# A hybrid decoder layer on one core: who scales the probability rows of head 2 in three units

## What is computed

```
p_c = masked_softmax(s_c, ...); o_cmp = einsum('bgqrc,bcgd->bgqrd', p_c, v_c)
p_s = masked_softmax(s_s, ...); o_slc = einsum('bgqrm,bgqmd->bgqrd', p_s, v_g)
p_w = masked_softmax(s_w, ...); o_win = einsum('bgqrk,bkgd->bgqrd', p_w, v_wb)
o_nsa = gates[..., 0:1] * o_cmp + gates[..., 1:2] * o_slc + gates[..., 2:3] * o_win
o_nsa = o_nsa * silu(nsa_z)
return x + einsum('bse,ed->bsd', concatenate([o_nsa, o_conv]), w_out)
```

## Time and profile before

| | us |
|---|---|
| median of 3 runs | 653.49 |
| lowest to highest | 653.38 to 653.90 |
| profiled execution | 654.13 |
| its span | 652.3 |
| PE busy in the span | 640.4 |
| DVE, ACT, POOL busy | 485.5, 378.1, 201.8 |

### The profile page before, as it was taken

One profiled execution on the slowest core, in us unless ns is written; L12 is line 12 of the kernel. 1 busy time (PEld: TensorE's weight loads), 2 busy tenths in 40 slices (PEclk: granted clock), 3 DMA queues, 4 the chain that ended last, 5 costly groups with the idle time before them and its releaser, 6 DMA issues.

```text
span 652.3 us, 10319 instructions
## 1 busy us (share of the span) xinstructions
PE 640.4 (98%) x3513; PEld 539.4 (83%) x3513; DVE 485.5 (74%) x1153; ACT 378.1 (58%) x872; POOL 201.8 (31%) x220
## 2 busy tenths in 40 slices
PE   9999999999999999999999999998999999999997
PEld 6889998888888888888888888886888878788876
DVE  4945979996755754776698867898887778787853
ACT  6754457564344354555666655778766655665651
POOL 3433304343432232322213312357642221311210
PEclk9999999999999999999999999999999999999999
DMA  8523102102111111111011010133311011011111
GB/s 314 159 57 115 40 27 60 46 27 81 39 44 44 38 33 41 42 30 36 16 34 33 17 33 17 50 97 118 109 34 65 33 34 65 33 33 50 48 34 65
DMA packets 20212, 37.35 MB, mean 57 GB/s; under 512 B 2880, under 2 KB 4288, under 8 KB 20160
## 3 DMA queue, kind: packets, MB, share of 16 engines
q1 hardware_dynamic: 20016, 36.68, 18.1%
q10 hardware_dynamic: 144, 0.00, 0.0%
HBM read 32.48 MB, written 4.19 MB: 56 GB/s over the span
## 4 chain that ended last, share of the span: by engine, by line
PE 83%; DVE 12%; issue 3%; ACT 2%; ACTq 0%; DVEq 0%
PE pf L1464 11%; PE pf L1465 10%; PE pf L1466 10%; PE tp L1774 6%; PE po L1754 5%; PE sc L1618 5%; PE sc L1617 4%; PE po L1755 4%; PE pj L1464 3%; PE pj L1465 3%; PE pj L1466 3%; PE sc L1464 3%; PE sc L1465 3%; PE sc L1466 3%; DVE sc L1371 2%
## 5 line engine op out<-in xcount | busy, mean ns | idle before, releaser
L963 ACT CAST pth<-tp 128x512 fp32r<-128x512 f32 (+1 forms) x148 | 86.9, 587 | 109.3 <-PE tp L1774 108.8
L1371 DVE CUSTOM_DVE_ANT_0 sc<-sc,maskb 128x64 f32<-128x64 f32 (+8 forms) x192 | 103.1, 561 | 46.7 <-PE sc L1618 45.8
L1393 DVE TENSOR_TENSOR ptl<-tp,pth 128x512 fp32r<-128x512 f32 x132 | 90.9, 689 | 24.7 <-ACT pth L963 24.1
L683 POOL TENSOR_SCALAR qp<-qp,precip,gate 128x64 f32<-128x64 f32 x64 | 42.1, 658 | 187.3 <-DVE precip L1361 187.1
L643 POOL TENSOR_TENSOR fl<-fraw,fh 128x512 fp32r<-128x512 f32 x40 | 54.1, 1353 | 97.1 <-ACT fh L808 97.1
L1464 PE MATMUL pf<-hh,fh 128*128 128x512 f32 x200 | 80.2, 401 | 2.6 <-DVE th L1331 1.6
L1465 PE MATMUL pf<-hl,fh 128*128 128x512 f32 x200 | 78.3, 391 | 0.0
L1466 PE MATMUL pf<-hh,fl 128*128 128x512 f32 x200 | 78.1, 391 | 0.0
L634 POOL TENSOR_TENSOR wl<-qp,wh 128x512 fp32r<-128x512 f32 (+1 forms) x33 | 49.4, 1520 | 87.6 <-ACT wh L723 84.0
L1774 PEld LDWEIGHTS tp<-idr,qpr 128*128 128x128 f32 (+1 forms) x592 | 61.7, 137 | 11.6 <-issue 2.2
L1774 PE MATMUL tp<-idr,qpr 128*128 128x128 f32 (+1 forms) x592 | 68.1, 238 | 1.0 <-DVE ptl L1393 0.3
(11 more groups left out here) (257 smaller groups left out, 1552.7 us busy)
## 6 DMA issues: line engine op xcount, KB each, us to landing
fraw<-in_wside SPq DMA_DIRECT2D x40, 256.0 KB, 2.7
qp<-in_wpack SPq DMA_DIRECT2D x28, 256.0 KB, 3.0
xo<-in_x SPq DMA_DIRECT2D x16, 256.0 KB, 2.8
out<-xo SPq DMA_DIRECT2D x16, 256.0 KB, 2.0
wor<-in_wout SPq DMA_DIRECT2D x12, 256.0 KB, 2.8
mixc<-in_xcm SPq DMA_DIRECT2D x4, 512.0 KB, 7.1
xlow<-in_xcm SPq DMA_DIRECT2D x3, 512.0 KB, 6.0
qp<-in_wpack SPq DMA_DIRECT2D x5, 224.0 KB, 2.5
```

What stands on the lines that cost most here:

```text
L963: nc.scalar.copy(pth[ptn % 2][0:r, :], tp[tpn % 2][0:r, :]).then_inc(pth_ready, 1)
L1371: return V.tensor_tensor_reduce(row, row, mask, -1.0, -NEG, ALU.add, ALU.min, most)
L1393: V.tensor_tensor(ptl[ptn % 2][:, :], tp[tpn % 2][:, :], pth[ptn % 2][:, :].bitcast(F32), ALU.subtract).then_inc(tp_read, 1)
```

## The change

In units 9 to 11 the scaling of head 2 goes the way of head 0. ACT_HEADS is replaced by a function of the job, act_heads(w), which gives (0, 2) for the jobs 18 to 23 and (0,) for all others; act_rows(w) counts the rows that ACT has scaled before job w. The waits on factor_ready, p_act and p_dve count accordingly. Nothing else is changed, and PE's instructions are the same in the same order.

```diff
-ACT_HEADS = (0,)
+def act_heads(w):
+
+    return (0, 2) if 9 <= w // 2 < 12 else (0,)
+
+def act_rows(w):
+
+    return sum(len(act_heads(v)) for v in range(w))
@@ ACT, step k
-                if 0 <= s < NS and s % 4 in ACT_HEADS:
-                    act.wait_ge(factor_ready, len(ACT_HEADS) * (s // 4) + ACT_HEADS.index(s % 4) + 1)
+                if 0 <= s < NS and s % 4 in act_heads(s // 4):
+                    act.wait_ge(factor_ready, act_rows(s // 4) + act_heads(s // 4).index(s % 4) + 1)
                     A(main_probs(s), main_probs(s), ACT.Copy, scale=precip[:, s % 4, 0:1]).then_inc(p_act, 1)
@@ DVE, scale(s)
-                if h in ACT_HEADS:
+                if h in act_heads(w):
                     V.tensor_tensor(factor, factor, main, ALU.mult).then_inc(factor_ready, 1)
@@ PE, first transposes of job n
-                    pe.wait_ge(p_act, len(ACT_HEADS) * (n + 1))
-                    pe.wait_ge(p_dve, (GH - len(ACT_HEADS)) * (n + 1))
+                    pe.wait_ge(p_act, act_rows(n + 1))
+                    pe.wait_ge(p_dve, GH * (n + 1) - act_rows(n + 1))
```

## The result

| | before | after |
|---|---|---|
| median of 9 runs each, same comparison, us | 653.83 | 655.40 |
| lowest to highest | 653.38 to 654.18 | 655.24 to 656.13 |
| span of the profiled run | 652.3 | 653.4 |

The ratio is 1.0025 with a 95% interval of 1.0016 to 1.0033: the change makes the kernel 1.6 us slower, 1.0 to 2.2 by the interval. The forecast was 655.5 us and a cost of 2.0. The two profiled spans differ by less, 1.1 us, because the profiled run after the change happened to be 0.7 us ahead before it reached the changed rows.

A forecast was written before the change was run, and what follows sets the result against it. PE, busy 640.4 of 652.3 us, was taken as the bound, so only its waits count. The terms 0.66 + 0.42 - 0.33 + 0.43 + 0.83 = +2.0 us on 653.49 gave 655.5 us, range 653.9 to 656.3.

The forecast's parts named there:

- Row 1: Steps 76 and 77: ACT's new row delays pth, oc and DVE's chain to th, costing PE +0.66 us near 424.
- Row 2: Steps 80 and 81: PE's first transpose of job 19 waits for ACT's new row, +0.42 us.
- Row 3: Steps 83 and 84: th starts earlier, L1336 again comes just behind POOL's wol; -0.33 us, bounds 0 and -1.43.
- Row 4: Steps 88 to 91: pth and ptl move later, PE's own waits absorb part; net +0.43 us, bounds 0 and +0.65.
- Row 5: Steps 92 to 94: ACT's new row delays the pth cast and an unbroken chain to PE's idle at 489.62; +0.83 us.
- Row 6: Steps 96 and 97: the pushed exponential is covered by the pth cast's 0.75 us wait for PE; cost 0.
- (a): Rival: L1336 wins the port in step 83, giving -1.43 in place of -0.33; 654.4 us, chance 0.20.
- (b): Rival: ACT's pushes are covered, so 1.55 us of the cost go; 654.0 us, no change, chance 0.12.
- (c): Rival: DVE is the bound, and all 2.8 us of its freed time come off; 650.7 us, chance 0.05.
- (d): Rival: Row 3 gains nothing and Row 4 costs its full 0.65; 656.0 us, chance 0.08.

The follow-up runs named there:

- e5: Of the change only job 18's row, against the kernel before; one run, 654.71 us.
- e3: Kernel before, with POOL's split of output-weight block 4 (step 83) made to wait until DVE's L1336 is done; 652.91 us, ratio 0.9983.
- e1: Kernel before, with DVE's one-column multiplication for the six rows and no added ACT work (rows stay unscaled); 653.06 us against 653.99, ratio 0.9988.
- e6: Of the change only job 20's row, against the kernel before; one run, 652.98 us.
- e9: Changed kernel, with ACT scaling head 2 ahead of the last pth cast of its step instead of behind it; 653.02 us against 654.11 of before, ratio 0.9984.
- e2: Changed kernel, but DVE scales all rows as before and ACT multiplies the six rows by 1.0; 655.69 us, ratio 1.0025 to the kernel before.
- e7: Of the change only job 21's row, against the kernel before; one run, 654.29 us.
- e8: Of the change only job 22's row, against the kernel before; 654.77 us, ratio 1.0013.

## Why the prediction held

**Direction and size.** The forecast was +2.0 us; timed it is +1.6 and in the trace +1.83. That 655.5 us met 655.40 is luck in part: the kernel before was timed 0.34 us slower in this comparison than the 653.49 I started from, and the cost was 0.4 smaller than forecast. The account by places held in sign at six of the seven; at 468, where nothing was forecast, a small gain appeared.

**Row 1 (+0.66 forecast, +0.55 measured).** The mechanism is the one described, and e5 gives it alone (+0.53). The step "from there ACT runs without a gap to pth" was mis-sized: that cast had waited about 0.1 us for PE's transposes, so it moved by less than 0.73. DVE's ptl waits 0.40 us for ACT now, and PE waits first for ot and then for th:

```profile
423.05 0.47 PE L1764 MATMUL po<-pth,val 128*128 128x512 f32 x1 [0.33 <-DVE ot L1429]
...
424.06 0.50 PE L1474 MATMUL pf<-hh,fh 128*128 128x512 f32 x1 [0.32 <-DVE th L1341]
```

I had looked for PE's idle at 424 to grow to 0.95; it shows as two waits instead, since the one for ot comes first and takes most of the new delay (0.50 of 0.53 us; PE's start at 424 adds the rest). The shift is the measure, not the length of a single wait.

**Row 2 (+0.42, +0.38).** Right. Of the 0.13 us that I added between a release and a matmul about half was there: ACT's row ends at 434.38 + 0.83 = 435.21, and PE's transposes start at 435.27.

**Row 3 (-0.33, -0.29).** Right in both its halves: the one-column multiplication waited for POOL, and L1336 lost again. e3 shows the 1.1 us that would have followed otherwise. The margin was 0.02 us and not the 0.09 that I had worked out, so an error of a tenth in that sum could have turned it, and that the sum fell on the right side is luck in part. The order itself is no chance of one run: th (447.40) and POOL's copies (447.39) both start when POOL's subtraction ends, and L1336 starts 0.00 to 0.02 us behind wol in e1, e6 and e9 too and takes 1.83 to 1.84 us.

**Row 4 (+0.43, +0.20).** The chain through ACT, ptl and PE is right. From its level ahead of 468 (-0.04) PE's delay rises to +0.65 at 475.28, 0.69 against a forecast of 0.65. What was mis-sized is how much PE's own waits take back behind it: 0.49 and not 0.22, because two more waits for ptl, near 478.5 and 480.8, had room for 0.10 and 0.15 us; e2 and e7 show the same 0.49 and 0.50. I had also overlooked what DVE's freed time in step 87 gives to POOL. POOL's timeline, first before, then after, and PE's weight load for the transposes behind it, after:

```profile
464.11 0.73 POOL L683 TENSOR_SCALAR qp<-qp,precip,gate 128x64 f32<-128x64 f32 x1 [4.54 <-DVE precip L1361]
...
464.06 0.39 POOL L693 TENSOR_SCALAR qp<-qp,precip,gate 128x64 f32<-128x64 f32 x1 [4.55 <-DVE precip L1371]
...
468.04 0.40 PEld L1784 LDWEIGHTS tp<-idr,qpr 128*128 128x128 f32 x4 [0.39 <-ACT qp L1001]
```

In the kernel before POOL's row took 0.73 us, for DVE's TENSOR_SCALAR of row 86 ran beside it. Now POOL's queue is 0.34 earlier. PE's first transposes of job 21 (468.21 in the kernel before) had waited for POOL's next compressed row. In e1 and e9 they come 0.34 us earlier; after the change only 0.13, for now they wait for ACT's scaled row of job 21. The forecast had this wait for the jobs 19 and 22 alone. But what PE gains there it waits for at 475, where DVE's chain sets the time: -0.11 is inside the +0.80, and in e1 -0.36 and +0.32 nearly cancel. A VectorE row that nobody waited for had held up POOL, and it was worth next to nothing in the end.

**Row 5 (+0.83, +0.99).** Right in size; e8 gives it alone: PE gains 0.16 at 480.8, from the DVE time freed in step 91, and loses 0.99 behind it, so +0.83 in all. The forecast had said that this freed time touches nothing; it is given back when PE waits for ACT. PE's wait for the scaled row (0.34) is inside the delay as said. The rest shows at 485 as a wait for ot (0.55), not at 489.62: the wait there stays at 0.3.

**Row 6 (0, 0).** No jump there; not tested alone.

**The rivals.** (a) is out for this kernel but real (e3). (b) is out by e2. (c) is out by e1. (d) is out: row 3 gave its gain, and row 4 kept 0.20.

## What to carry to other kernels

When work is moved to the engine with more idle time, look at what stands behind it in that engine's queue and who waits for that: 3.9 us more on a ScalarE that is 58% busy cost 1.6 us, and the same work a cast earlier, in time spent waiting for TensorE, cost nothing. Freed time pays only where the freed engine is what TensorE waits for at that moment; here 2.8 us of it gave 0.7 to 0.9. Where two engines hold each other up, changing which of them comes first can be worth more than taking work away: one wait added to POOL gave 1.0 to 1.1 us.

## What was new about the hardware

A multiplication of a single column can take as long as the POOL instruction that runs beside it has left: 0.67 us in step 83 and up to 1.20 us in step 89 of the kernel after, against 0.16 where POOL is idle. The timeline of DVE and POOL, first where POOL is idle until 464.06, then step 89:

```profile
464.00 0.16 DVE L1374 TENSOR_TENSOR precip<-precip,gate 128x1 f32<-128x1 f32 x1
...
471.21 1.20 DVE L1374 TENSOR_TENSOR precip<-precip,gate 128x1 f32<-128x1 f32 x1
471.07 1.32 POOL L706 TENSOR_TENSOR wol<-wor,woh 128x512 fp32r<-128x512 f32 x1
```

Of the 38 such multiplications in this kernel nine took over 0.3 us, and each of them ended 0.01 to 0.02 us behind a subtraction of POOL. And it goes the other way: POOL's row of 64 columns takes 0.39 us alone and 0.73 beside a VectorE row of 640 columns. The busy sums count these waits as work.
